# A mixture-of-experts stage: the residual in DRAM and a ninth weight slot, earlier key products, and weight rows of 16 KB

## What is computed

```python
for l in range(DEPTH):                       # DEPTH = 2
    h = rms_norm(x, attn_norm[l])
    ...                                      # three mixers side by side
    x = x + y @ w_out[l]
    x = x + hier_moe(rms_norm(x, ffn_norm[l]), w_group[l], b_group[l],
                     w_expert[l], b_expert[l], w1[l], w3[l], w2[l])
```

## Time and profile before

| | us |
|---|---|
| median of three runs | 2955.46 |
| lowest and highest | 2948.49, 2960.16 |
| the profiled execution, its own time | 2950.76 |
| its span, first to last instruction | 2949.0 |
| PE busy | 2824.7 |
| DVE busy | 1110.5 |
| ACT busy | 663.0 |
| POOL busy | 511.6 |
| mean granted TensorE clock, of full speed | 0.992 |

### The profile page before, as it was taken

How to read it: one execution, slowest core, us unless ns; L and a number is a source line. 1 busy time by engine, 2 the same in 40 slices (tenths; PEclk the granted TensorE clock), 3 DMA queues, 4 the chain that set the end, 5 groups by cost and what they waited for, 6 DMA issues and landing times.

```text
span 2949.0 us, 32180 instructions
## 1 busy us (share of the span) xinstructions
PE 2824.7 (96%) x12444; PEld 1903.5 (65%) x12444; DVE 1110.5 (38%) x2248; ACT 663.0 (22%) x1512; POOL 511.6 (17%) x785
## 2 busy tenths in 40 slices
PE   8999999799999987999999999999999999999998
PEld 4565543255655432685566688888686575788887
DVE  4543311155433111445432333354446432334354
ACT  3333110033331101105512211101206512211100
POOL 3101111131111111113300022201114410122201
PEclk9999999999999999999999999999999999999999
DMA  3206799831067998420011122222220020222222
GB/s 133 75 29 255 274 417 418 361 135 60 29 257 310 416 419 349 179 86 30 30 60 55 62 93 93 82 79 93 86 86 29 23 93 29 86 86 86 72 85 87
DMA packets 126418, 422.12 MB, mean 143 GB/s; under 512 B 10480, under 2 KB 14704, under 8 KB 103088
## 3 DMA queue, kind: packets, MB, share of 16 engines
q1 hardware_dynamic: 112944, 387.01, 34.4%
q0 software_dynamic: 12736, 30.84, 2.8%
q10 hardware_dynamic: 576, 2.10, 0.2%
HBM read 408.63 MB, written 27.26 MB: 148 GB/s over the span
## 4 chain that ended last, share of the span: by engine, by line
PE 75%; issue 9%; SPq 7%; DMA 3%; DVE 2%; POOL 1%; ACT 1%; POOLq 1%; DVEq 0%; ACTq 0%
PE ps L2520 35%; PE ps L427 5%; PE ps L2753 5%; PE ps L1760 4%; SPq L1694 4%; PE ps L1108 4%; PE ps L2726 3%; DMA ring_feat<-in_w 2%; PE ps L1328 2%; PE ps L2627 2%; PE ps L2773 2%; PE ps L3087 2%; PE ps L1801 2%; SPq L1692 1%; SPq L1690 1%
## 5 line engine op out<-in xcount | busy, mean ns | idle before, releaser
L427 PE MATMUL ps<-ring_feat 128*128 128x512 f32 (+2 forms) x704 | 275.5, 546 | 5.3 <-DMA ring_feat<-in_w_lat 3.2
L2520 PE MATMUL ps<-ring_feat 128*128 128x256 f32 x1216 | 276.9, 380 | 0.8 <-ACT big L287 0.8
L2520 PE MATMUL ps<-big 128*128 128x256 f32 x1200 | 268.2, 379 | 0.0
L2520 PEld LDWEIGHTS ps<-ring_feat 128*128 128x128 f32 x1216 | 231.5, 190 | 32.8 <-issue 2.1
L2520 PEld LDWEIGHTS ps<-big 128*128 128x128 f32 x1200 | 228.5, 190 | 30.5
L427 PEld LDWEIGHTS ps<-ring_feat 128*128 128x128 f32 x704 | 133.2, 192 | 131.1 <-issue 93.8
L2753 PE MATMUL ps<-ring_feat 128*128 128x512 f32 x320 | 139.4, 593 | 0.7 <-ACT ring_feat L2151 0.7
L2520 PE MATMUL ps<-tmp 128*128 128x256 f32 x576 | 128.2, 379 | 0.0
L2520 PE MATMUL ps<-ring_feat,tmp 128*128 128x256 f32 x544 | 126.6, 379 | 0.0
L2520 PEld LDWEIGHTS ps<-tmp 128*128 128x128 f32 x576 | 109.7, 190 | 14.6
L1108 PE MATMUL ps<-ring_feat 128*128 128x512 f32 x256 | 113.7, 596 | 0.0
(11 more groups left out here) (495 smaller groups left out, 4638.1 us busy)
## 6 DMA issues: line engine op xcount, KB each, us to landing
big<-in_w SPq DMA_DIRECT2D x36, 2048.0 KB, 20.3
ring_feat<-in_w SPq DMA_DIRECT2D x36, 2048.0 KB, 26.7
ring_feat<-in_w_gate_up SPq DMA_DIRECT2D x22, 2048.0 KB, 8.0
ring_feat<-in_w_mix_in SPq DMA_DIRECT2D x12, 2048.0 KB, 8.1
ring_feat<-in_w_down SPq DMA_DIRECT2D x12, 1536.0 KB, 6.7
par<-in_w SPq DMA_DIRECT2D x12, 1024.0 KB, 22.4
e_spare<-in_w SPq DMA_DIRECT2D x12, 1024.0 KB, 22.0
tmp<-in_w_mem_kv SPq DMA_DIRECT2D x6, 2048.0 KB, 26.9
```

The lines of the kernel that those rows point to most:

```text
L427: yield T.matmul(bank, lhs(k), rhs(k), start=k == 0, stop=k == n - 1)
L2520: m = T.matmul(to, lhs[:, j, :], rhs[:, j, :], start=start and j == 0, stop=stop and j == chunks - 1)
```

## The change

1. **x leaves SBUF during the experts.** After it has scaled a tile for the experts, ACT stores the tile of x to a new DRAM tensor `x_saved`, on its own queue (`share_tile`). The place of x becomes slot 8 of nine (`X_HOME`). Its first chunk, chunk 8, is loaded when all four stores of x have landed and all four stores to `normed` too. All chunks now lie in slot c % 9, and `expert_loads` loads chunk c when chunk c - 9 has been used. When pair 14's down product is done, SP loads the four tiles of x back, behind the last expert and key/value loads and ahead of the next stage's weights. DVE's adds in `combine` wait for all four.
2. **Key products move forward.** The first bank of key products is opened before the last tile is turned. Its k-steps 0 and 1 go ahead of that turn, 2 and 3 behind the counts of tile 2, 4 to 7 to where 0 to 3 were, and the second product's k-steps 0 and 1 to where 4 and 5 were.
3. **Rows of 16 KB.** `w13`, `w2` and `w_mem_kv` are laid out on the host such that every chunk of 2 MB is 128 rows of 16 KB. PARTED chunks take two loads (12 + 4 KB and 14 + 2 KB a row) and not three. The loads of the spill blocks, which take one expert, are split to match, with the expert's number as pair and parity (two more DVE operations of 15 columns).
4. **First tile scaled first.** In `entry_norm` after a combine, ACT scales tile 0 before it squares tile 1.
5. The positions' load signals `const_loaded`, and `pos_loaded` is gone.

```diff
@@ entry_norm
+            add_waits = added is not None
             for t in range(TT):
                 if name == "act":
                     if added is None:
                         eng.wait_ge(tile_loaded[t], 16)
+                    late_tile = add_waits and t == 1
+                    if late_tile:
+                        scale_x(eng, j, 0, buf)
                     square_x(eng, j + t, t, buf, 0 if added is None else added + t + 1)
-                    if t:
+                    if t and not late_tile:
                         scale_x(eng, j + t - 1, t - 1, buf)
@@ first_out, after the last tile
             slot_done(name)
+            take(name, "ring")
+            keys = first_keys_w(name)
+            first_keys_loaded(name, eng)
+            key_q = at["first_keys"] = key_open(name, 0, (gate_steps, 2 * l + 2))
+            key_products(name, key_q, 0, keys, range(2))
             turn_raw(name, eng, y0, TT - 1)
             share_tile(name, eng, j0, TT - 1, buf)
             place_tile(name, eng, l, TT - 2)
+            key_products(name, key_q, 0, keys, range(2, 4))
             table_begin(name, eng, l)
             route_tile(name, eng, l, j0, TT - 1)
@@ share_tile
             if name == "act":
                 scale_x(eng, j0 + t, t, buf)
+                eng.dma_start(a["x_saved"][t * P:(t + 1) * P, :], x[:, t, :]).then_inc(x_moved, 16)
@@ router
+            key_products(name, at["first_keys"], 0, w, range(4, KC))
+            key_read(name, eng, l, 0, 0, at["first_keys"], counted=False)
             key_q = key_open(name, 0)
-            first_keys_loaded(name, eng)
-            key_products(name, key_q, 0, w, range(4))
...
-            key_products(name, key_q, 0, w, range(4, 6))
+            key_products(name, key_q, 1, w, range(2))
...
-            key_products(name, key_q, 0, w, range(6, KC))
-            key_read(name, eng, l, 0, 0, key_q)
-            key_job(name, eng, l, 0, 1, w)
+            key_products(name, key_q, 1, w, range(2, KC))
+            key_read(name, eng, l, 0, 1, key_q)
@@ slots
-        SLOTS, PARTED, OTHER_W, FEAT, KEY_W = 8, (3, 4), 5, 6, 7
+        SLOTS, PARTED, OTHER_W, FEAT, KEY_W, X_HOME = 9, (3, 4), 5, 6, 7, 8
@@ e_slot
+            if s == X_HOME:
+                return x_all[:, 0:UP]
@@ load_chunk
-            pair = slice(2 * p, 2 * p + 2)
-            src = a["w2"][l, pair] if part == DOWN0 else a["w13"][l, pair, :, part * UP_HALF:(part + 1) * UP_HALF]
+            src = (a["w2"][l, p] if part == DOWN0 else a["w13"][l, p, part]).rearrange("p e n -> p (e n)")
             if s in PARTED:
-                sp.dma_start(main[:, 0:UP_HALF], src[0]).then_inc(chunk_loaded[s], 16)
-                sp.dma_start(main[:, UP_HALF:UP_HALF + split], src[1][:, 0:split]).then_inc(chunk_loaded[s], 16)
-                sp.dma_start(rows[:, at:at + UP_HALF - split], src[1][:, split:]).then_inc(chunk_loaded[s], 16)
+                sp.dma_start(main[:, 0:UP_HALF + split], src[:, 0:UP_HALF + split]).then_inc(chunk_loaded[s], 16)
+                sp.dma_start(rows[:, at:at + UP_HALF - split], src[:, UP_HALF + split:]).then_inc(chunk_loaded[s], 16)
@@ expert_loads, at its end
             load_kv(sp, l, 3)
+            sp.wait_ge(down_full, (l + 1) * PAIRS - 1)
+            x_tiles = a["x_saved"].rearrange("(t p) d -> p t d", p=P)
+            for t in range(TT):
+                sp.dma_start(x[:, t, :], x_tiles[:, t, :]).then_inc(x_moved, 16)
@@ combine, add(t)
+                eng.wait_ge(x_moved, 32 * TT * (l + 1))
                 eng.wait_ge(tile_loaded[t], 16 * (l + 2))
@@ SP's program, before expert_loads
                 sp.wait_ge(bank_full, feat_free[l])
                 load_chunk(sp, l, FEAT)
+                sp.wait_ge(normed_first, 16 * (l + 1))
+                sp.wait_ge(normed_rest, 16 * (TT - 1) * (l + 1))
+                sp.wait_ge(x_moved, 16 * TT * (2 * l + 1))
+                load_chunk(sp, l, X_HOME)
                 expert_loads(sp, l)
@@ host layout
+    def by_chunk(w):
+        return np.ascontiguousarray(w.reshape(LAYERS, P, KC, 4, 512).transpose(0, 3, 1, 2, 4))
+    w13 = w13.reshape(LAYERS, PAIRS, 2, 2, KC // 2, P, 2 * D_EXP).transpose(0, 1, 3, 5, 2, 4, 6)
+    w2 = v["w2"].reshape(LAYERS, PAIRS, 2, 2, P, D).transpose(0, 1, 4, 2, 3, 5)
```

More of the change, by code:

```diff
@@ L163, in program @@
         normed_first, normed_rest = sem("normed_first"), sem("normed_rest")
-        chunk_loaded = [sem(f"expert_slot{s}_loaded") for s in range(8)]
+        chunk_loaded = [sem(f"expert_slot{s}_loaded") for s in range(9)]
+        x_moved = sem("x_saved_and_back")
         up_half = sem("up_half")
@@ L1598, in router @@
         def router(name, eng, l):
-            take(name, "ring")
             w = first_keys_w(name)
@@ L1674, in chunk_count @@
             s = c % SLOTS
-            return (48 if s in PARTED else 16) * (l * len(range(s, CHUNKS, SLOTS)) + c // SLOTS + 1)
+            return (32 if s in PARTED else 16) * (l * len(range(s, CHUNKS, SLOTS)) + c // SLOTS + 1)
         e_x = [view(tmp, s * D, D) for s in range(2)]
@@ L3619, in _ @@
                 assert n % 2 == l % 2
-                load(a["w_mem_kv"][l][:, :, 0:512], KC, 512)
+                load(a["w_mem_kv"][l, 0], KC, 512)
                 load_kv(sp, l, 1)
@@ L3747, in host_layout @@
         w_mix_out=chunks(np.concatenate([v["a_w_out_2"], v["b_w_out_2"]])),
[L3748 removed]
+        w_mem_kv=by_chunk(chunks(v["x_wkv_2"])), w_mem_q=chunks(w_q), w_mem_o=chunks(v["x_wo_2"]),
         w_gate_up=chunks(gu), w_down=chunks(v["w_down_2"]))
```

55 lines of the change are left out of this document (31 added, 24 removed).

## The result

The changed kernel took 2961.69 us (median of 6 runs, 2960.12 to 2964.28), the kernel before 2952.34 us on the same chip (2947.98 to 2960.16). The ratio is **1.0033, 95% interval 1.0021 to 1.0045**: 9.7 us slower (0.0033 x 2952), where the forecast was 4.6 us faster. The measured time lies in the range that I had stated, but the difference is clear of the noise and has the other sign. The changed kernel measured again beside the last experiments gave 1.0033 (1.0023 to 1.0044). Two executions among the experiments, one of e2 (3322 us) and one of e4 (8531 us), lie far above all the others and are left out of the ratios.

The account below looks back on a forecast made before the run. Bound: the last expert weights landing, set by when the DMA engines become full for good plus remaining bytes over rate. Slot -10.0, restart +8.0, rows -4.6, reading back +2.0 gave -4.6 us: median 2951 us, range 2936 to 2966.

Parts of the forecast that it names:

- (b): Measured distance per layer from the restart to PE's first record of the last down product; before: 241.7 and 244.0 us.
- the restart: Moment when the load waiting for pair 0's first half product starts; forecast +3 us in layer 1, +5 in layer 2.
- (a): Measured distance per layer from PE's first record on the last tile's turn to the restart; before: 26.8 and 22.2 us.
- reading back: Loading x from DRAM at the experts' end, claimed mostly to fit into free DMA time: +1 us a layer, bounds 0 and 5.0.
- (c): Measured distance per layer from the last down product to the next stage's first product; before: 28.0 and 29.3 us.
- The full stretch: Expert weight loading with all DMA engines full: slot -5.0 us a layer, 16 KB rows -2.3, rate 423 GB/s.
- The store: Last normalized tile's store beside x's fourth copy: +2 us in layer 2, nothing in layer 1, where the table is later.
- The gather beside chunk 8: First gather of pair 0's rows sharing the DMA engines with chunk 8's load: +3 us a layer, bounds 0 and 6.9.
- 6.4 us of fixed work: Between PE's turn of pair 0's rows and the restart: the restart follows by this constant time.
- Key products: Moved forward in the router: gain 0, the gather being late next; clock effect 4.7 us a layer only for the range.
- First tile: Stage start after a combine: scaling tile 0 sooner gains 0, since PE's clock-keeping products cover it; 2 us at most.
- B: Rival, chance 0.13: first rows so late, behind x's copy and chunk 8, that the slot costs more: +15 us, 2971 us.

Follow-up runs that it names:

- e2: The kernel before with only the moved key products added: ratio 0.9990 to the kernel before.
- e4: The changed kernel with one wait more, so that chunk 8 is loaded only after pair 0's gathered rows have landed: 0.9997 of the kernel before.
- e3: The kernel before with 16 KB rows and x both saved and read back, eight slots, nothing loaded into x's place: 1.0022 of the kernel before.
- e6: The kernel before with 16 KB rows and x saved but never read back, eight slots: 0.9998 of the kernel before.
- e12: The changed kernel itself, measured again beside the last experiments: 1.0033 of the kernel before.
- e1: The kernel before with only the 16 KB row layouts added, eight slots, no copies of x: 0.9983 of the kernel before.
- e11: The changed kernel with the key products put back where they were before: 1.0032 of the kernel before.
- e9: The kernel before with 16 KB rows, moved key products and the first tile scaled first: 0.9966 of the kernel before.
- e7: The changed kernel with both chunk 8 and the chunk into the features' place loaded behind the first gather: 0.9987 of the kernel before.
- e10: The changed kernel with chunk 8 and the features' chunk behind the first gather and half of x read back behind the first results: 0.9974 of before.
- e5: The kernel before with 16 KB rows and moved key products, without the ninth slot and the copies of x: 0.9964 of the kernel before.
- e8: The changed kernel with chunk 8 behind the first gather and half of x read back behind the first results: 0.9992 of the kernel before.

## Why the prediction was wrong

In the terms of the sum, both layers together: slot and rows were put at -14.6 us and (b) fell by 14.1; the restart was put at +8.0 and (a) grew by 17.1; reading back was put at +2.0 and cost 7.4 ((c) of e3 against e6). Another 1.5 us of (c) and -1.9 us elsewhere stood in no term.

**The full stretch: right.** I had -5.0 for the slot and -2.3 for the rows, -7.3 a layer. (b) fell by 7.7 and 6.4 (7.4 and 8.7 in e12). The rows alone gave 2.9 and 3.4, the slot 4.2 and 2.6 beyond e3 (e4 against e3: 3.8 and 4.7). The rate formed from 2 KB and 8 KB rows said 423 GB/s; e1 has 423.

**The restart: the step that failed.** The sum had "+3 us in the first layer, +2 + 3 = +5 us in the second". It was +6.2 and +10.8.
- *The store.* I took 2 us, near the lower end of 1.25 to 7, "since only 0.52 MB are added to some 4.7 MB under way". It was +4.5 in layer 2 (7.5 to 12.0), above the middle of that span. For layer 1 I wrote that nothing is added, since the table is later. The store had landed 5.3 us ahead of the gather there; its landing went from 6.1 to 12.2, past the table, and the gather, counted from the last turn, came 1.7 us later (16.75 against 15.07).
- *The gather beside chunk 8.* I took 3 of 0 to 6.9; it was +4.0 and +4.1, and e4 takes it away again with one wait. The Trainium skill (DMA: Bandwidth & Descriptors, Queues, rings and completion order) has the engines take turns between queues packet by packet, from which I worked out 0. The trace does not agree with that estimate (+4.0 and +4.1 us). The same passage of the Trainium skill says that an engine drains a whole packet, typically some 9 to 17 descriptors, before it switches, so 0 did not follow from it. Whether the length of the rows matters is open: chunk 8 in shorter rows beside the gather was not run.
- *"6.4 us of fixed work"* from the rows' turn to the restart. It was 8.0 and 8.8 us: PE came out of its wait at half clock, and turned the rows in 1.97 us in place of 1.04. Beside these, 1.1 us of the gather's delay in layer 1 lay under PE's key products. Layer 1: 1.7 + 4.0 - 1.1 + 1.6 = 6.2. Layer 2: 4.5 + 4.1 + 2.4 = 11.0, measured 10.8.

**Key products: counted at 0, worth 3 us alone, and no gain shown here.** The step "the gather, not PE, is late next" holds for the changed kernel (e11). What I had only as a bound, 4.7 us a layer for the clock, is in e2 the gain: (a) of layer 1 from 26.8 to 23.0. In the changed kernel PE waits 1.3 us longer with them; whether the restart comes sooner, the runs leave open.

**Reading x back: failed by size.** I had +1 a layer, since 6.4 us of engine time were free. (c) grew by 6.4 and 2.5. In layer 2 the reading back itself is 0.9 us of that (e3 against e6), so my 1 us was right there; 2.1 to 2.2 us stand in e1 and e6 too. In layer 1 it is the whole (6.5 us, e3 against e6). There I had priced the delay of the results' loads behind x, but not that of the last scatter, which those loads wait for. The mean share of 0.29 or 0.33 hid it: the scatter was under way for 8.0 us from 580.11, while the 16 engines together were busy for a third of 579 to 588 us.

**First tile: right within what e9 can tell**, 0. The rest was not run by itself.

**The rivals.** The place and the mechanism of B, copy and chunk in front of store and gather, are what happened, with the store 4.5 and not 7 us later and (b) fully paid. Its point of decision, restart and reading back together over 7.3 us a layer, was passed in both layers ((a) and (c) together grew by 12.6 and 13.3). Its other sign, a gap before the restart as empty as before, did not come (share 0.59 against 0.32). I gave it 0.13 with the reason that only 8 us of bytes had to be moved in the hole: bytes over rate is the wrong measure for two small transfers on which everything waits. Of the signs I named, chunk 8 landing in the hole, the rate (424, within 420 to 424), and PE's wait for a gather came; PE's waits for weights from 325 to 580 us shrank by 8.1 us (17.2 to 9.1) where I had 5. The load into x's place was issued at 321.76 and 914.69 us where I had about 320 and 907; the restart was 5.5 us later where I had 3, and 16.6 where I had 5, of which 5.7 were carried over into layer 2.

## What to carry to other kernels

Here a transfer that was "hidden in a gap" delayed every small transfer on the critical path that landed in the same gap. List these first (here a store, a gather, a scatter), read their landings in the trace with and without neighbours, and put the bulk load behind them by a wait (e4: 10.6 us for one line). Price a small transfer's delay by landings seen under load, not by added bytes over the rate, and take a gap's free time by what lands in it, not by the mean share of the engines. Split a bundled change: here two of its parts gained 10.6 us together, and with the ninth slot and the copies added the kernel was some 20 us slower than with these two.

## What the runs showed that I had not expected

- Beside the last normalized store one chunk of 2.10 MB is under way in every kernel (issued 4.5 us ahead of it), and in all but e7 and e10 the chunk into the features' place is issued 0.5 to 2.1 us behind it. The store landed after 5.4 to 7.5 us with both chunks and no copy of x (nine of the ten stores of before, e1, e2, e5 and e9; the tenth took 10.6), after 7.1 to 8.2 with the 0.52 MB copy of x and without the features' chunk (e7, e10), and after 11.7 to 12.8 with the copy and both chunks (all 14 of the changed kernel, e3, e4, e6, e8, e11 and e12).
- The rows of 16 KB have a price that nothing here pays: in the full stretch the gathers land later. The page's part 6 of before has 10.5 us, that of e2 10.3, that of e1 14.7, and the eleven other profiles with the same rows have 14.5 to 14.9:

```profile
tmp<-normed,route_i POOLq DMA_INDIRECT x32, 14.7
```

  PE doesn't wait for these gathers; a kernel with less time between gather and use might.
- The last scatter of layer 1 lands in 3.6 us (e6), or in 8.0 (e3, and the changed kernel, where the DMA engines are meanwhile busy for a third of the time on average). Behind the reading back, the next stage's first weights (1.7 MB, issued at 570.80 us) land after 16.8 us in the changed kernel, where e6 has 11.7. Which engine holds it was not looked into.
- PE's granted clock fell to the lower level in the router of layer 1 before, of layer 2 in e1, and of layer 1 in e3, with the router's instructions as they were before. With the key products moved, (a) was 22.4 to 23.6 us in all ten layers of e2, e5, e7, e9 and e10; with them as before, in before and e1, 22.2 to 26.9. In the changed kernel PE's waits of 9.9 and 9.0 us cost 1.6 and 2.4 us more behind them, in work at half clock.
